# Last squares of each norm summed on TensorE, its sums and spreads moved among products, and the output stored in five pieces

## The reference, cut to what matters

```
def rms_norm(x, w):
    y = x * lax.rsqrt(jnp.mean(x * x, axis=-1, keepdims=True) + EPS)
    return y * w

# first block
n = rms_norm(h, attn_norm_w)                       # norm 0
h = h + concat([y_attn, y_ret]) @ w_out
m = rms_norm(h, ffn_norm_w)                        # norm 1
h = h + (silu(m @ w_gate) * (m @ w_up)) @ w_down   # first FFN
# second block
a = rms_norm(h, g_mix)                             # norm 2, mixing block
h = h + merged @ w_out_2
c = rms_norm(h, g_cross)                           # norm 3, cross attention on a memory
h = h + cross_attention(c, mem) 
f = rms_norm(h, g_ffn)                             # norm 4
h = h + (silu(gate) * up) @ w_down_2               # second FFN
return rms_norm(h, g_final)                        # norm 5, output
```

## Time and profile before

| | before |
|---|---|
| median of 3 runs | 2806.79 us (2806.77 to 2807.2) |
| profiled execution, its own time | 2803.61 us |
| its span in the trace | 2801.8 us |
| granted TensorE clock, mean | 0.988 |
| PE, PEld, DVE, ACT, POOL busy | 97%, 78%, 63%, 38%, 54% |
| DMA | mean 56 GB/s |

### The profile page before, as it was taken

The page is one execution under the profiler, slowest core; times in us unless marked ns, Lnnn a source line. Parts: engine busy times, 40 slices in busy tenths (PEclk is TensorE's granted clock), DMA queues, the critical chain, the costliest instruction groups (busy, mean ns, idle before and its releaser), DMA issues.

```text
span 2801.8 us, 37256 instructions
## 1 busy us (share of the span) xinstructions
PE 2704.8 (97%) x13668; PEld 2184.5 (78%) x13668; DVE 1752.6 (63%) x2657; ACT 1060.5 (38%) x2069; POOL 1510.8 (54%) x1144
## 2 busy tenths in 40 slices
PE   7999999999999999999999899999998999999997
PEld 6777788778888888787766688878777788888886
DVE  6776664677777777713367731143368777677777
ACT  5644431344444444424344410021243444443443
POOL 3322333377878788542222244446513778787884
PEclk9999999999999999999999999999999999999998
DMA  3010111111212111210100011132101112121112
GB/s 134 31 38 31 36 51 63 46 57 57 64 57 68 54 61 52 107 61 31 39 31 32 31 46 53 53 120 63 66 23 45 57 57 62 59 65 56 58 53 79
DMA packets 102710, 157.17 MB, mean 56 GB/s; under 512 B 6928, under 2 KB 60688, under 8 KB 101392
## 3 DMA queue, kind: packets, MB, share of 16 engines
q1 hardware_dynamic: 95296, 129.00, 14.5%
q10 hardware_dynamic: 7248, 25.95, 2.4%
HBM read 146.54 MB, written 8.39 MB: 55 GB/s over the span
## 4 chain that ended last, share of the span: by engine, by line
PE 85%; DVE 9%; ACT 2%; POOL 2%; issue 2%; DMA 0%; POOLq 0%; ACTq 0%; DVEq 0%
PE PS L1271 13%; PE PS L1273 13%; PE PS L1272 13%; PE PS L945 11%; PE PS L947 10%; PE PS L946 10%; PE PS L985 1%; PE PS L1050 1%; PE PS L982 1%; PE PS L983 1%; PE PS L1039 1%; PE PS L1065 1%; PE PS L1419 1%; PE PS L1425 1%; DVE XL L2374 1%
## 5 line engine op out<-in xcount | busy, mean ns | idle before, releaser
L782 POOL TENSOR_TENSOR WH<-WRAW,CST 128x512 fp32r<-128x512 f32 x204 | 228.3, 1119 | 874.7 <-PE PS L947 745.8
L945 PE MATMUL PS<-XH,WH 128*128 128x512 f32 x1248 | 513.1, 411 | 4.4 <-DVE XL L2374 2.8
L947 PE MATMUL PS<-XH,WL 128*128 128x512 f32 x1248 | 489.9, 393 | 0.0
L946 PE MATMUL PS<-XL,WH 128*128 128x512 f32 x1248 | 489.3, 392 | 0.0
L2821 DVE TENSOR_TENSOR H<-H,PS 128x512 f32<-128x512 f32 x560 | 367.0, 682 | 43.7 <-PE PS L1273 43.6
L817 POOL TENSOR_TENSOR WL<-WRAW,WH 128x512 fp32r<-128x512 f32 x174 | 251.2, 1445 | 107.4 <-ACT WH L1937 106.7
L945 PEld LDWEIGHTS PS<-XH,WH 128*128 128x128 f32 x1248 | 235.4, 189 | 84.3 <-issue 38.0
L784 POOL TENSOR_TENSOR WL<-WRAW,WH 128x512 fp32r<-128x512 f32 x204 | 268.6, 1317 | 16.0
L947 PEld LDWEIGHTS PS<-XH,WL 128*128 128x128 f32 x1248 | 235.6, 189 | 51.8
L946 PEld LDWEIGHTS PS<-XL,WH 128*128 128x128 f32 x1248 | 236.0, 189 | 42.2 <-issue 0.5
L1271 PE MATMUL PS<-XH,WH 128*128 128x512 f32 x640 | 249.4, 390 | 3.0 <-POOL WL L817 2.9
(11 more groups left out here) (355 smaller groups left out, 5401.9 us busy)
## 6 DMA issues: line engine op xcount, KB each, us to landing
WRAW<-ws SPq DMA_DIRECT2D x104, 512.0 KB, 3.4
WRAW<-ws SPq DMA_DIRECT2D x120, 256.0 KB, 2.7
XX<-ws SPq DMA_DIRECT2D x108, 256.0 KB, 2.7
RAWX<-ws SPq DMA_DIRECT2D x56, 256.0 KB, 2.7
H<-xT ACTq DMA_DIRECT2D x4, 1024.0 KB, 10.6
H<-xT ACTq DMA_DIRECT2D x2, 2048.0 KB, 11.0
h_spill<-H ACTq DMA_DIRECT2D x1, 4096.0 KB, 11.1
H<-h_spill ACTq DMA_DIRECT2D x4, 1024.0 KB, 8.0
```

The costliest lines, as they stand in the source:

```text
L782: pool.tensor_tensor(WH[:, j, c], WRAW[:, j, c], ONES[:, 0:1].to_broadcast((P, 512)), ALU.mult).then_inc(hi_split, 1)
L945: pe.matmul(out, WH[:, j, w], rh(kt), start=(n == 0), stop=False)
L946: pe.matmul(out, WH[:, j, w], rl(kt), start=False, stop=False)
L947: last = pe.matmul(out, WL[:, j, w], rh(kt), start=False, stop=(n == len(kts) - 1))
```

## The change

**Sums.** The last square of each half (numbers 13 or 14, and 15; at norms 2 and 5 the last four, 12 to 15) is no longer added to `ACC` by DVE. PE sums it straight from `SQ` with four more matmuls (`norm_square`) that accumulate in the same columns of `MB`. There are 14 such groups of four.

**Places on PE.** At norms 1, 3 and 4 the sums and spread of the first half now stand inside the last unit (ahead of `kt` 3 and 6); the second half's sums stand at `kt` 2 of the next block (in the memory unit at norm 3) and its spread at `kt` 6, where it was `kt` 3 for the FFN and the mixing block. In `last_outputs` the first half's spread stands behind output 13, the second half's sums behind output 14, its squares behind 14 and 15 and, at norm 2, at `kt` 1 and 3 of `first_units`.

**Places on DVE and ACT.** DVE makes steps 0 and 1 ahead of its last addition to `H` (`last_result`, at step 2; in `last_outputs` ahead of outputs 14 and 15), ACT squares that last tile ahead of high part 1. The second half's reciprocal stands at step 5 (was 2). DVE waits for all of POOL's low parts (`w_low`) ahead of the additions of `last_outputs`. The order of the last four results of cross attention's output changes (`cross_tile`).

**Tail.** The second half's reciprocal stands ahead of final steps 2 to 15, and SP stores five pieces (4, 4, 4, 2 and 2 tiles) where ACT stored four.

```diff
 # SP
+            for n, (h, first, last) in enumerate(((0, 0, 4), (0, 4, 8), (1, 0, 4), (1, 4, 6), (1, 6, 8))):
+                sp.wait_ge(final, 8 * h + last)
+                sp.dma_start(outT[:, first:last, half(h)], H[:, first:last, half(h)]).then_inc(y_out, 16)
+            sp.wait_ge(y_out, 80)
...
 # PE
             def norm_sums(k, h):
 
-                pe.wait_ge(summed, 2 * h + 2 if not k else 16 * k + 4 if h else 16 * k - 4 if k in (2, 5) else 16 * k + 3)
+                pe.wait_ge(summed, 2 * h + 2 if not k else SUM_BASE[k] + (8 + 4 * h if k in (2, 5) else 13 + h))
                 for b in range(4 * h, 4 * h + 4):
-                    last = pe.matmul(PS[:, MB, b:b + 1], ACC[:, b // 4, blk(b % 4)], ONES[:, 0:1], start=True, stop=True)
...
+            def norm_square(k, h, n):
+
+                pe.wait_ge(squared, SQ_BASE[k] + n + 1)
+                end = h == 0 or n == 15
+                for b in range(4):
+                    last = pe.matmul(PS[:, MB, 4 * h + b:4 * h + b + 1], SQ[:, n % 2, blk(b)], ONES[:, 0:1], start=False,
+                                     stop=end and b == 3)
+                last.then_inc(col_sum if end else sq_read, 1)
...
+            def first_half_norm(k, n, sums_at, spread_at):
+
+                def hook(kt):
+                    if kt == sums_at:
+                        norm_sums(k, 0)
+                        norm_square(k, 0, n)
+                    if kt == spread_at:
+                        norm_spread(k, 0)
+                return hook
...
 # PE, ffn: plain(0), then last_outputs
-                            if b == 0 and h == 0 and kt == 3:
+                            if b == 0 and h == 0 and kt == 2:
+                                norm_sums(k, 1)
+                                norm_square(k, 1, 15)
+                            if b == 0 and h == 0 and kt == 6:
                                 norm_spread(k, 1)
...
                         if o == 11:
                             norm_sums(k + 1, 0)
+                        if o == 13:
+                            norm_spread(k + 1, 0)
+                        if o == 14:
+                            norm_sums(k + 1, 1)
+                        if o >= 14:
+                            norm_square(k + 1, 1, o - 2)
...
+            def mix_norm(h, kt):
+
+                if h == 0 and kt in (1, 3):
+                    norm_square(2, 1, 14 + kt // 2)
+                if (h, kt) == (0, 6):
+                    norm_spread(2, 1)
...
 # ACT, ffn
                 for n in range(16):
                     kt, h = n % 8, n // 8
-                    if n == 2:
+                    if n == 1:
+                        last_square()
+                    if n == 4:
                         norm_root(k, 1)
...
-                            if o == 12:
+                            if o == 11:
                                 norm_root(k + 1, 0)
...
 # DVE, ffn: steps, then last_outputs
                         if n == 2:
+                            last_result()
+                        if n == 5:
                             norm_inverse(k, 1)
...
-                    base = 16 * (k + 1) + 4 - 16
-                    for o in range(17):
-                        if o < 16:
-                            t, h = down_tile(o)
-                            dve.wait_ge(prod, bases + DONE["last", LAST, o])
-                            dve.tensor_tensor(H[:, t, half(h)], H[:, t, half(h)], PS[:, o % 4], ALU.add).then_inc(h_added, 1)
-                        if o >= 9:
...
+                    dve.wait_ge(w_low, N_SLOT * (f + 1))
+                    for o in range(16):
+                        if o >= 14:
+
+                            if f:
+                                final_step(o - 14)
+                            else:
+                                norm_step(2, V_GMIX, o - 14)
+                        t, h = down_tile(o)
+                        dve.wait_ge(prod, bases + DONE["last", LAST, o])
+                        dve.tensor_tensor(H[:, t, half(h)], H[:, t, half(h)], PS[:, o % 4], ALU.add).then_inc(h_added, 1)
+                        if 9 <= o < 13:
...
-                        if o == 13:
+                        if o == 12:
                             norm_inverse(k + 1, 0)
...
 # DVE, tail
-            for h in range(2):
-                dve.wait_ge(spread, 10 + h + 1)
-                for kt in range(KT):
-                    if (h, kt) == (0, 2):
-                        norm_inverse(5, 1)
...
+            norm_inverse(5, 1)
+            for n in range(2, 16):
+                final_step(n)
```

More of the change, by code:

```diff
@@ L547, in r_bank @@
             return (3, 1, 3, 1)[n] if n < 4 else n
+        SQ_BASE = {k: 16 * k - 12 for k in range(1, 6)}
+        SUM_BASE = {1: 4, 2: 18, 3: 30, 4: 44, 5: 58}
         def unit_done(eng, u):
@@ L1645, in _ @@
             pe.wait_ge(pt_ready, 96)
-            for n in range(4):
+            for n in range(3):
                 for second in (1, 0):
@@ L1650, in _ @@
                             cross_out(n, second, h)
-            norm_spread(4, 0)
-            norm_sums(4, 1)
+            for h in range(2):
+                cross_out(3, 1, h, first_half_norm(4, 13, 3, None) if h else None)
+                cross_out(3, 0, h, first_half_norm(4, 13, None, 2) if h else None)
             ffn(1, U_FFN2, XS_F2, 4)
+            norm_square(5, 1, 14)
+            norm_square(5, 1, 15)
             norm_spread(5, 1)
@@ L1682, in norm_high @@
                 for n in range(first, last):
[L1683 removed]
+                    if n == 4 and k != 3:
                         norm_root(k, 1)
@@ L1914, in residual @@
                 nsq.end(3)
-                last_squares(u0, k)
+                for n in range(12, 15):
+                    t, h = n // 2, n % 2
+                    bank = 2 * (t % 2) + h
+                    square(k, n, t, h, bank, uses[u0 + t][bank])
+                norm_root(k, 0)
             def vm_copy(n):
@@ L2325, in _ @@
             split_cross(1)
-            for n in range(4):
-                u = U_CO + n
-                for second in (1, 0):
-                    for h in range(2):
-                        bank = 4 + h if second else 2 * (u % 2) + h
-                        square(2 * n + second, h, bank, uses[u][bank])
-                        if (n, second, h) == (3, 0, 0):
-                            norm_root(4, 0)
-            ffn(1, 4)
-            norm_root(5, 1)
-            for q in range(4):
-                h, kts = q // 2, slice(4 * (q % 2), 4 * (q % 2) + 4)
-                act.wait_ge(final, 4 * q + 4)
-                act.dma_start(outT[:, kts, half(h)], H[:, kts, half(h)]).then_inc(y_out, 16)
-            act.wait_ge(y_out, 64)
+            for n in range(15):
+                t, h = cross_tile(n)
+                u = U_CO + t // 2
+                bank = 4 + h if t % 2 else 2 * (u % 2) + h
+                square(4, n, t, h, bank, uses[u][bank])
+                if n == 13:
+                    norm_root(4, 0)
+            ffn(1, 4, last_square4)
+            norm_root(5, 1)
         @block.vector
@@ L2687, in residual, with last_result1, last_result4, final_step @@
                     nsm.end(3)
-                    for t in (6, 7):
-                        for h in range(2):
-                            bank = 2 * ((u0 + t) % 2) + h
-                            add_result(t, h, bank, uses[u0 + t][bank])
-                            add_squares()
-                            if (t, h) == (7, 0):
-                                norm_inverse(k, 0)
-            def ffn(f, k, gain):
+                    for n in range(12, 15):
+                        t, h = n // 2, n % 2
+                        bank = 2 * (t % 2) + h
+                        add_result(t, h, bank, uses[u0 + t][bank])
+                        if n < 14:
+                            add_squares(k, n, h)
+                    norm_inverse(k, 0)
+            def last_result1():
+                add_result(7, 1, 3, uses[U_WO1 + 7][3])
+            def last_result4():
+                add_squares(4, 14, 1)
+                add_result(6, 1, 3, uses[U_CO + 3][3])
+            def final_step(n):
+                kt, h = n % 8, n // 8
+                if kt == 0:
+                    dve.wait_ge(spread, 10 + h + 1)
+                x = H[:, kt, half(h)]
+                dve.scalar_tensor_tensor(out=x, in0=x, scalar=v(V_GFIN + kt), in1=PS[:, OB + h], op0=ALU.mult,
+                                         op1=ALU.mult).then_inc(final, 1)
+            def ffn(f, k, gain, last_result):
                 hid, bases = 44 * f, N_DONE * f
@@ L2867, in _ @@
             residual(U_WO1, 1)
-            ffn(0, 1, V_F1)
-            norm_scale(2, V_GMIX)
+            ffn(0, 1, V_F1, last_result1)
+            for n in range(2, 17):
+                norm_step(2, V_GMIX, n)
             def soft2(s):
@@ L3034, in _ @@
                     bank = 2 * (u % 2) + h
+                    if (t, h) == (7, 1):
```

(8 more changed lines are left out.)

181 lines of the change are left out of this document (88 added, 93 removed).

## The result

The change made the kernel slower: 2827.03 us (median of 4, 2825.15 to 2827.85) against 2806.99 (median of 4), +20.0 us, ratio 1.0069 with a 95% interval from 1.0052 to 1.0087. I had forecast 2820.2 and a range up to 2826.0: the direction was right, the size (13.4 of 20.0) too small by a third, and the time lies 1 us above the range. The profiled execution took 2827.48 us, its span is 2825.6.

What follows compares the result with a forecast made beforehand. PE was 97% busy, but norms 1 and 4 were priced by DVE's step 8. Five norms summed to +11.7 us, with one clock fall +13.4; added to the median, 2820.2 us, range 2810 to 2826 (8 in 10).

Steps and rivals of the forecast that it cites:

- What bounds the kernel: PE busy 97% of the span; behind norm 1 the chain runs through DVE, ACT and POOL, so step 8's start decides.
- the term of the clock: Behind PE's waits at norm 4: one clock fall slows eight products now on the path, costing 1.6 us.
- Norm 1 and norm 4: FFN entries: step 8 starts later, +2.6 us (1.8 to 3.1) at norm 1 and +2.8 (1.9 to 3.4) at norm 4.
- The recorded sum: The prediction's addition over the five norms, 2.6 + 2.8 - 0.9 + 2.8 + 4.4 = 11.7 us, before the clock.
- Norm 2: Ahead of the mixing block: later sums, squares and second spread, then DVE pacing the second half; +2.8 us (+1.3 to +4.5).
- Both steps of the argument: At norm 2: second spread at 1190.0 against 1184.58 before, then step 8 at 1191.3 against 1187.79.
- Norm 3: Ahead of cross attention: PE's waits shrink by more than two square blocks cost; -0.9 us (-1.3 to +0.3).
- Norm 5: At the end: wait for POOL, PE's waits and later scalings delay the output; +4.4 us (3.8 to 4.8).
- the table rule: At norms 2 and 5: a drain after the root's table load delays each inverse 1.4 us; 2823 in all, 3 in 100.
- The range: Whole kernel: 2810 to 2826 us at 8 in 10; the forecast's own range is 2814 to 2824.
- slower still: Clock falls at norms 1, 2, 4 and in the tail, at upper bounds for contention; 2825 to 2828 us, 14 in 100.
- The signs: Profile after: norm 1's first scale to step 8 14.7 us or more; longer POOL wait; norm 5 waits over 1 us.

Runs made afterwards that it cites:

- spread_kt4: Changed kernel with the second spread at kt 4 instead of kt 6 of the first FFN block; 2817.05 us (1.0043).
- the fill: Throwaway PE products added to the changed kernel in PE's waits at norms 1 and 4; 2822.75 us ahead of the second FFN block only, 2818.81 ahead of both.
- clock_fill: Changed kernel with throwaway PE products in its waits ahead of both the first and second FFN blocks at norms 1 and 4; 2818.81 us (1.0044).
- n25_before: Changed kernel with norms 2 and 5 as in the kernel before, five output pieces kept; 2817.09 us (1.0039).
- low_late: Changed kernel with DVE's wait for POOL's last low parts moved from ahead of the sixteen last additions to ahead of the fifteenth; 2824.73 us (1.0066).
- tail_early: Changed kernel with the last reciprocal moved behind final step 4; 2823.46 us (1.0062).
- before's second trace: The kernel before, unchanged, profiled once more; 2805.00 us, one execution, where its first trace took 2803.61.

## Why the prediction was wrong, point by point

**What bounds the kernel** was right. What norms 1 and 4 are worth was to be read from when step 8 starts: spread_kt4 moved it and got its time.

**The step that failed is the term of the clock:** "I count one such fall", eight products, 1.6 us (the sum has 1.7 for it). The reasoning named the mechanism (products ahead of the spread are now on the path, and slow after a wait), but priced one fall. The runs show four on the path: 1.6 ahead of step 8 at norm 1, 2.7 at norm 4 (twelve products, and slower sums), and 1.8 and 2.2 behind the longer wait for POOL, 8.3 in all. The kernel before pays a part of that itself: 0.0 or 1.4 behind norm 1 and 0.9 or 1.5 behind norm 4 in its two traces (0.0 and 0.6 against -0.9 with the fill). Net the change costs 5.4 to 7.4 by the clock, three to four times the term, and this makes up 3.7 to 5.7 of the 6.6 that were missing. The rest stands at norm 3 (1.5 instead of -0.9, with one more fall) and at norm 2 (3.7 instead of 2.8). One fall by itself was priced rightly, at 1.6. What the forecast had wrong is how many of them cost time: it read one window at norm 4 and did not ask at which of the four places PE's products would be on the path. The omission behind it: the forecast let PE enter the FFN block as soon as its own work and column 0 allowed, and did not see that the block's start waits for the bank that the late addition frees. With the waits of 2.63 and 4.30 in the sum, two falls would have had to be counted ahead of step 8.

**Norm 1 and norm 4** without the clock: 2.2 and 3.0 late at step 8 in clock_fill. The recorded sum was 2.6 (1.8 to 3.1) and 2.8 (1.9 to 3.4). Right.

**Norm 2:** forecast +2.8 (1.3 to 4.5), measured 3.7 against the first trace and 4.3 against the second, with the 0.5 from the row above. Both steps of the argument hold. The second spread at 1198.45 is at 1191.1 without the 7.3 of lateness on entry (forecast 1190.0), and step 8 follows at 1192.2 (forecast 1191.3):

```profile
1198.45 1.05 PE L1026 MATMUL PS<-CST,STAT 128*128 128x128 f32 x8
...
1199.54 0.75 DVE L2445 SCALAR_TENSOR_TENSOR XX<-H,VEC,PS 128x512 f32<-128x512 f32 x1 [0.80 <-PE PS L1026]
```

What is new there is that the norm differs from trace to trace: the row is 2.4 to 3.3 in most of them, and 6.6 and 7.5 in two where the clock stayed low for longer. Where the last 0.9 over the forecast goes is not shown.

**Norm 3:** forecast -0.9, measured 1.5 to 1.7, or 0.0 in n25_before, low_late and tail_early. The changed kernel shows a wait of PE there that before has not, of 1.9 for POOL's split of a weight (1960 to 2030):

```profile
PE PS L995 <- POOL WL L800: 1.9, 1, 1.9
```

n25_before has this wait too and no loss, and its clock is 1.00 from 1986 to 1990, where the changed kernel's is 0.57 from 1992 to 1996. So the 1.6 goes with a fall of the clock. The other traces say the same: the clock fell some 5 us ahead of step 8 of norm 3 in all eight traces that lose 1.5 to 1.7 there, and stayed at 1.00 in the three (n25_before, low_late, tail_early) that lose nothing. That the fall decides was not tried by itself here; why the two blocks did not bring the forecast's 0.9 otherwise stays open.

**Norm 5:** forecast +4.4 (3.8 to 4.8), measured 4.2 from the entry on, with its parts as described: the wait for POOL (1.4, forecast 1.3), PE's waits ahead of the sums and the spread, scalings behind the root, and output pieces that change nothing. Without the 19.6 of lateness on entry the sums start at 2777.8 and the fourteen scalings at 2791.8, to the tenth where the forecast had put them.

**The table load** at norms 2 and 5: load 1.28 and the root's activations right behind it in the trace of after too (1177.67, 1178.96 and 1179.07), so the table rule's further 1.4 did not show, and the 3 in 100 was well placed.

```profile
1177.67 1.28 ACT L1715 ACT_TABLE_LOAD   x1
...
1178.96 0.20 ACT L1715 ACTIVATE STAT<-VEC 128x1 f32<-128x1 f32 x1
1179.07 0.25 ACT L1721 ACTIVATE STAT<-PS,VEC 128x4 f32<-128x4 f32 x1
```

**The range** had a case, "slower still", with 14 in 100 and 2825 to 2828, in which the clock falls at several norms. That is nearest to what happened, though it was at norms 1, 3 and 4 that more falls cost time, and not at upper bounds for contention. A range to 2826 cut it.

**The signs** came out as named, but for the wait ahead of the last norm's sums (0.91, not over 1): 16.8 us from the first scaling to step 8 at norm 1 (14.7 or more), a wait for POOL of 6.5 (over 2.4), and at norm 5 7.9 us from the second half's sums to the first output issue, where before it was 2.9.

## What to carry to other kernels

Where a change lengthens or adds a wait of TensorE by a few microseconds, price the slow products behind each such wait, not one for the kernel: here each cost 1.6 to 2.7 us, a quarter to two thirds of the wait. First look at whether they are on the path: the same fall at norm 1 cost nothing before, while DVE paced step 8. A result that frees a buffer (the last addition to `H`) has readers beyond the chain one is shortening: list every semaphore that it raises before putting work ahead of it. And an operation put later in a busy engine's order costs the whole stretch of that order if someone else's half of the work starts with it; one number, `kt` 6 to 4, was worth about 7 us, a part of it by the clock.

## What the runs showed of the hardware

- Idle time of TensorE is dearer than it looks: 24 products whose results are thrown away, put in a wait of 6.5 us, took 1.8 and 2.2 us off the path behind it in the traces, and two and four longer ones (fp32) in waits of 2.63 and 4.30 us took off 1.6 and 2.7.
- DVE's subtraction of 128x512 from two inputs in SBUF took 1.78 us beside an operation of POOL and 0.68 without, and POOL's start, 1.7 earlier relative to DVE in before's second trace, cost it 1.2 us (the growth at "rest of first FFN"). The Trainium skill (GPSIMD Engine Reference, Specifications, row SBUF interfaces) names contention with DVE instructions that have two SBUF inputs; the trace agrees.
- The kernel before is not one time: its two traces differ by 1.4 us in all, but by -1.6 to +1.4 at single places. At both of these ends the granted clock is at one level in one trace and at the other in the next. A place's loss of 1 to 2 us is only shown by several traces.
